# Two double norms of a three-block kernel: each square computed once, into a lent PSUM tile, both sums on VectorE

## The chip, the cores and the metric

The kernel runs on one core of one Trainium2 chip. The metric is the device time of one execution in microseconds, as the median of several runs; lower is better.

## The reference, cut to what matters

Three transformer-like blocks follow one another on 1024 positions of width 1024, in float32 (plus 16 meta positions in the first). Between blocks stand two norms in a row, with nothing between them: block 1 ends in a norm and block 2 begins with one, and block 2 ends in a norm and block 3 begins with one.

```python
h = h + jnp.square(jax.nn.relu(hn @ w_up[layer])) @ w_down[layer]
out = rms_norm(h, norm_final_w)
...
h = rmsnorm(x, ln1_g[l])
p = jnp.einsum('bsd,dn->bsn', h, w_in[l])
...
x = x + jnp.einsum('bsf,fd->bsd', hidden, w_down[l])
return rmsnorm(x, g_final)
...
h = rms_norm_3(x, norm1_pre) * (1.0 + scale1) + shift1
```

A norm divides by the root of the mean square over the 1024 features and multiplies by a gain g. Two in a row need two sums for each position: the sum of x squared, and the sum of (g x) squared, where g is the gain of the first of the two.

## The kernel before, in words

**Layout.** Features lie on the partitions, in eight tiles X[:, k, :] of 128 x 1024 (1024 positions in the free dimension). A weight block of 128 outputs is multiplied by all eight tiles. For precision each float32 operand is split into a high part and the rest: ScalarE rounds (`hh` for activations, `whi` for weights), VectorE or GpSimd subtracts (`hl`, `wlo`), and TensorE does three products per tile and half: whi with high, whi with low, wlo with high (L581, L582, L584). A product of eight tiles (`job`, L590) is 48 matmuls of 512 columns; one of four tiles, as in the second half of an MLP, is 24.

**PSUM.** There are three product tiles of 128 x 1024, `ps[0]` to `ps[2]`, taken in turn by `take` (L545), and a fourth, `misc`, for small things. `take` waits until the former holder of the slot is "free", that is, read by VectorE or ScalarE; it is called at the start of each product, ahead of its first matmul.

**Order.** Each engine has its own function with its program written out in order, and waits on the counts of the others. Weights come through a ring of four raw tiles on SyncE's queue; ScalarE casts a weight (`highs`, L1218) when the product two places earlier is done, and GpSimd makes the low part behind it (`lows`, L2605). `behind(name)` stands in ScalarE's and GpSimd's programs where that work is due.

**The two places.** Each of the first two MLPs ends in eight products of four tiles, one for each tile of X: dn7_0 to dn7_7 in block 1, fdn5_0 to fdn5_7 in block 2. VectorE adds product j to X (`to_x`, L2073). Then `on_last(j - 1)` follows on the engines, for the tile before:

- ScalarE (L1477, L1701): `high` makes hh (L1300), `square` writes x squared into T[0] (L1245; for tile 0 into T[2], L1237), and `square_b` writes (g x) squared into RT (L1253; for tile 0 into T[1], L1249).
- VectorE (L2148, L2418): `weigh` makes hl (L1871), and `square_sum` adds T[0] to T[2] (L1880, "acc").
- GpSimd (`square_sum_b`, L2624, drawn by L2616): adds RT to T[1] ("accb").

T[0] and RT have one buffer each: ScalarE's square k waits for acc k-1, and its scaled square k waits for accb k-1.

Behind the last product TensorE does the first projection of the next block (gg0 in block 2, zv0 in block 3: `job`, L865 and L1128), which waits tile by tile for hl. Then come `sums` (L667): for each of eight blocks of 128 positions, T[2] against a column of ones, and the same for T[1]. Float32 makes two matmuls of each, 16 for acc (L671) and 16 for accb (L676). The next projection (gv0, zv1) follows, and in it the factors are spread over the partitions (`spread_misc`).

Other norms (n1, n2, n4) have one sum and use `square` and `square_sum` without g.

Of the kernel before, what the change touches and what calls it, by code (L numbers as in the profile page):

```python
# [12 lines left out]
ACT = mybir.ActivationFunctionType  # L13
# [3 lines left out]
P = 128  # L17
# [227 lines left out]
def build(nc, d, out):  # L245
    ctx = ExitStack()
    with ctx:
# [43 lines left out]
        rms = const("rms", [P, 40])  # L291
        gprod = const("gprod", [P, 16])
        adat = const("adat", [P, 2, P])
        cols = const("cols", [P, NCOL])
# [241 lines left out]
        def tensor(e):  # L536
# [6 lines left out]
            one, two = rms[:, 8:16], rms[:, 32:40]  # L543

            def take(g):  # L545

                n = turn[0] % 3
                turn[0] += 1
                if held[n]:
                    q.wait_ge(*freed(held[n]))  # L550
                held[n], slot[g] = g, n
                return ps[n]
# [279 lines left out]
            def mlp(up, dn, sizes, htok, norm=None, nlast=None, step=None):  # L832

                def norm_in(k):
                    if k == 5:
                        spread_misc(norm + " sp", one, dv(norm + " r1"))

                n = 0
                for what, g, j in mlp_plan(up, dn, sizes):
                    if what == "up":  # L840
                        f = 4 * g + j
                        if norm or f > 2:
                            job(f"{up}{f}", hhs, hls, htok, 8, between=norm_in if norm and f == 1 else None)
                        if step:
                            step(n)
                        if norm and f == 0:
                            sums(norm, nlast)
                    elif norm or (g, j) != (len(sizes) - 1, 7):
                        s_ = 4 * (g % 2)
                        if norm or (g, j) != (len(sizes) - 1, 6):  # L850
                            job(f"{dn}{g}_{j}", ghs, gls, lambda k: [po(f"{up}lo{4 * g + k - s_}")], sizes[g], k0=s_)
                        else:
                            halves([f"{dn}{g}_6", f"{dn}{g}_7"], ghs, gls, lambda k, hf: [po(f"{up}lo{4 * g + k - s_}")], sizes[g], k0=s_, between=tail)
                        if step:
                            step(n)
                    n += 1

            mlp("up", "dn", [4] * 8, lambda k: [dv(f"hl2 {k}")], "n2", dv("n2 acc7"), step=row_step)
            row_step(-1)

# [5 lines left out]
            q.wait_ge(*dv("mod"))  # L866
            sums("n3", dv("n3 acc7"), po("n3 accb7"))
            job("gv0", hhs, hls, h3, 8, between=lambda k: k == 6 and spread_misc("n3 sp", two, dv("n3 r12"), dv("n3 s2")))
# [241 lines left out]
            for n, (what, g, j) in enumerate(mlp_plan("fup", "fdn", SIZES2)):  # L1110
                if what == "up":
                    m = FIRST2[g] + j
                    job(f"fupa{m}", hhs, hls, lambda k: [dv(f"hl4 {k}")], 8)
                    if m == 0:
                        q.wait_ge(*ac("rx rt"))
                        sums("n4", dv("n4 acc7"))
                    job(f"fupb{m}", hhs, hls, lambda k: [dv(f"hl4 {k}")], 8,
                        between=None if m else lambda k: k == 5 and spread_misc("n4 sp", one, dv("n4 r1")))
                else:
                    s_ = 4 * (g % 2)  # L1120
                    job(f"fdn{g}_{j}", ghs, gls, lambda k: [po(f"fuplo{FIRST2[g] + k - s_}")], SIZES2[g], k0=s_)
                row2_step(n)


            def h5(k):
                return [dv(f"hl5 {k}")]

            job("zv0", hhs, hls, h5, 8)  # L1128
            sums("n5", dv("n5 acc7"), po("n5 accb7"))
            job("zv1", hhs, hls, h5, 8, between=lambda k: k == 5 and spread_misc("n5 sp", two, dv("n5 r12"), dv("b43")))  # L1130
# [81 lines left out]
        def scalar(e):  # L1212
# [18 lines left out]

            def square(n, k, x, *tok, g=None):

                for t in tok:
                    q.wait_ge(*t)
                if k == 0:
                    e.activation(T[2][:], x, ACT.Square).then_inc(*ac.inc(f"{n} sq0"))  # L1237
                else:
                    if g is None:
                        if k > 2:  # L1240
                            q.wait_ge(*either(f"{n} acc{k - 2}"))
                    elif k > 1:
                        q.wait_ge(*either(f"{n} acc{k - 1}"))
                    b = T[(k - 1) % 2] if g is None else T[0]
                    e.activation(b[:], x, ACT.Square).then_inc(*ac.inc(f"{n} sq{k}"))  # L1245

            def square_b(n, k, x, g):
                if k == 0:
                    e.activation(T[1][:], x, ACT.Square, scale=g).then_inc(*ac.inc(f"{n} sqb0"))  # L1249
                else:  # L1250
                    if k > 1:
                        q.wait_ge(*po(f"{n} accb{k - 1}"))
                    e.activation(RT[:], x, ACT.Square, scale=g).then_inc(*ac.inc(f"{n} sqb{k}"))  # L1253

# [222 lines left out]
            def on_last3(m):  # L1477
                high(f"hh3 {m}", X[:, m, :], HH[:, m, :], dv(f"dn x7 {m}"), *([pe("up31")] if m == 0 else []), scale=gprod[:, m:m + 1])
                if m == 0:
                    q.wait_ge(*po("uplo31"))  # L1480
                square("n3", m, X[:, m, :], g=True)
                square_b("n3", m, X[:, m, :], col("norm_final", m))

# [4 lines left out]
            root("n3", 1024, double=True)  # L1488
            to_rt("n3", po("n3 accb7"))
            behind("gv0")  # L1490
# [210 lines left out]
            def on_last5(m):  # L1701
                high(f"hh5 {m}", X[:, m, :], HH[:, m, :], dv(f"fdn x5 {m}"), *([pe("fupb21")] if m == 0 else []), scale=gprod[:, 8 + m:9 + m])
                if m == 0:
                    q.wait_ge(*po("fuplo21"))
                square("n5", m, X[:, m, :], g=True)
                square_b("n5", m, X[:, m, :], col("g_final", m))

# [25 lines left out]
            root("n5", 1024, double=True)  # L1733
            to_rt("n5", po("n5 accb7"))
            behind("zv1")
# [115 lines left out]
        def vector(e):  # L1851
# [20 lines left out]

            def square_sum(n, k, g=None):
                if k == 0:
                    return
                b = T[(k - 1) % 2] if g is None else T[0]
                q.wait_ge(*ac(f"{n} sq{k}"))
                if k > 1:
                    q.wait_ge(*either(f"{n} acc{k - 1}"))
                e.tensor_tensor(T[2][:], T[2][:], b[:], ADD).then_inc(*dv.inc(f"{n} acc{k}"))  # L1880

# [31 lines left out]
            q.wait_ge(*dv.now())  # L1913
            tt(gprod[:, 0:8], col("norm_final", 0, 8), col("ln1", 0, 8), MUL, "gprod")
            q.wait_ge(*dma["meta"]("meta"))
            for k in range(8):
# [231 lines left out]
            def on_last3(m):  # L2148
                if m == 0:
                    q.wait_ge(*pe("up31"))  # L2150
                weigh("hl3", m, gprod[:, m:m + 1])
                square_sum("n3", m, g=True)

# [264 lines left out]
            def on_last5(m):  # L2418
                if m == 0:
                    q.wait_ge(*pe("fupb21"))  # L2420
                weigh("hl5", m, gprod[:, 8 + m:9 + m])
                square_sum("n5", m, g=True)

# [111 lines left out]
            for m in range(6):  # L2535
                square_sum("nm", m)
                if m == 0:
                    q.wait_ge(*pe("n5 one"))
                    for k in range(8):
                        q.wait_ge(*ac(f"n5 sqb7"))  # L2540
                        stt(X[:, k, :], X[:, k, :], col("g_final", k), ps[slot["n5 one"]][:], MUL, MUL, f"x5n {k}", *(("free n5 one",) if k == 7 else ()))
# [57 lines left out]
        def gpsimd(e):  # L2599
# [23 lines left out]

            def square_sum_b(n, k):  # L2624
                if k:
                    q.wait_ge(*ac(f"{n} sqb{k}"))
                    q.wait_ge(*po.now())
                    tt(T[1][:], T[1][:], RT[:], ADD, f"{n} accb{k}")

            def low(n, x, hi, dst, tok):  # L2630
# [45 lines left out]

            def mlp(up, dn, sizes, step=None, on_last=None, late=1):
                n = 0
                for what, g, j in mlp_plan(up, dn, sizes):
# [5 lines left out]
                    if what == "up" and 4 * g + j >= late:  # L2685
                        for f in (range(late + 1) if 4 * g + j == late else [4 * g + j]):
                            sl = 4 * (f // 4 % 2) + f % 4
                            low(f"{up}lo{f}", T[f % 3][:], GH[:, sl, :], GL[:, sl, :], ac(f"{up}hi{f}"))
                    elif on_last and g == len(sizes) - 1 and j:
                        on_last(j - 1)  # L2690
                if on_last:
                    on_last(7)

# [5 lines left out]

            mlp("up", "dn", [4] * 8, row_step, lambda m: square_sum_b("n3", m))  # L2700

# [73 lines left out]
            for n, (what, g, j) in enumerate(mlp_plan("fup", "fdn", SIZES2)):  # L2775
# [10 lines left out]
                else:  # L2786
                    behind(f"fdn{g}_{j}")
                    row2_step(n, f"fdn{g}_{j}")
                    if g == 5 and j:
                        square_sum_b("n5", j - 1)  # L2790
            square_sum_b("n5", 7)


# [382 lines left out]
```

## Time and profile before

| what | us |
|---|---|
| median of 3 runs (lowest, highest) | 3523.36 (3521.64, 3528.19) |
| the profiled execution | 3526.7 |
| its span, first to last instruction | 3523.8 |
| TensorE matmul busy | 3431.2 (97%) |
| VectorE busy | 1588.2 (45%) |
| ScalarE busy | 1002.8 (28%) |
| GpSimd busy | 1308.9 (37%) |

The mean granted clock of TensorE over the span is 0.987 of full speed. Matmuls are pipelined: the record of one of 512 columns lasts about 0.39 us, while starts are about 0.23 us apart. Busy time of TensorE is therefore no measure of what it could still gain; starts and idle times are. In the rows, "[1.81 <-DVE HL L1871]" means that the engine was idle for 1.81 us before this instruction and that VectorE's instruction of line 1871, which writes HL, released it. PEclk is the granted clock in a stretch as a share of full speed (2.4 GHz).

### The profile page before, as it was taken

What the parts mean: (1) busy time and instruction counts of PE and PEld (TensorE: products, weight loads), DVE (VectorE), ACT (ScalarE), POOL (GpSimd) and SP (SyncE); (2) the same over time, 40 slices, a digit from 0 to 9 for tenths busy, and PEclk for the clock granted to TensorE, in tenths of its full rate; (3) what the DMA queues carried; (4) which work ended last, traced back from release to release, by engine and by line L of the source; (5) the groups of instructions that cost most, each with busy time, mean ns of one, the idle gap of its engine ahead of it and who ended that gap; (6) DMA issues with size and microseconds to landing.
All of it is one profiled execution on the core that took longest, in us unless ns stands there. A gap on an engine that the chain in (4) does not pass through costs nothing.

```text
span 3523.8 us, 39083 instructions
## 1 busy us (share of the span) xinstructions
PE 3431.2 (97%) x16810; PEld 2792.9 (79%) x16810; DVE 1588.2 (45%) x1630; ACT 1002.8 (28%) x1457; POOL 1308.9 (37%) x682
## 2 busy tenths in 40 slices
PE   8999999999999999998999999999999999999997
PEld 6888888888888878765788888888877778888886
DVE  5553343333333468475455545445554531222224
ACT  5432221111111421475232222212422432222222
POOL 3112334444444423213324344344433543333333
PEclk9999999999999999999999999999999999999998
DMA  3112312222222211110212133132211111111113
GB/s 109 37 60 72 108 48 90 88 87 89 89 87 79 93 66 48 49 58 1 84 48 72 62 100 96 63 99 87 73 42 37 70 51 51 49 48 48 48 50 121
DMA packets 89432, 242.93 MB, mean 69 GB/s; under 512 B 13334, under 2 KB 20262, under 8 KB 89132
## 3 DMA queue, kind: packets, MB, share of 16 engines
q1 hardware_dynamic: 89260, 240.44, 20.6%
q8 instruction: 132, 2.16, 0.2%
q14 instruction: 40, 0.33, 0.0%
HBM read 222.40 MB, written 18.00 MB: 68 GB/s over the span
## 4 chain that ended last, share of the span: by engine, by line
PE 90%; DVE 5%; ACT 3%; POOL 2%; issue 0%; DMA 0%; SPq 0%; DVEq 0%; ACTq 0%
PE ps L581 27%; PE ps L582 27%; PE ps L584 27%; POOL wlo L2610 1%; PE ps L751 1%; PE ps L968 1%; DVE T L1855 1%; PE ps L1017 1%; PE ps L1001 1%; DVE P L2266 1%; ACT T L1554 0%; POOL GL L2616 0%; PE ps L954 0%; PE ps L932 0%; PE ps L609 0%; PE ps L611 0%
## 5 line engine op out<-in xcount | busy, mean ns | idle before, releaser
L2610 POOL TENSOR_TENSOR wlo<-raw,whi 128x1024 fp32r<-128x1024 f32 (+3 forms) x367 | 697.7, 1901 | 1669.1 <-ACT whi L1227 1669.1
L581 PE MATMUL ps<-HH,whi 128*128 128x512 f32 (+2 forms) x2736 | 1083.6, 396 | 20.2 <-POOL wlo L2610 7.3
L582 PE MATMUL ps<-HL,whi 128*128 128x512 f32 (+2 forms) x2736 | 1071.0, 391 | 0.0
L584 PE MATMUL ps<-HH,wlo 128*128 128x512 f32 (+2 forms) x2736 | 848.2, 391 | 0.0
L1227 ACT ACTIVATE whi<-raw 128x1024 fp32r<-128x1024 f32 (+3 forms) x367 | 309.8, 844 | 1645.9 <-PE ps L584 1453.3
L581 PEld LDWEIGHTS ps<-HH,whi 128*128 128x128 f32 (+2 forms) x2736 | 514.1, 188 | 134.1 <-issue 7.2
L584 PEld LDWEIGHTS ps<-HH,wlo 128*128 128x128 f32 (+2 forms) x2736 | 513.6, 188 | 112.3 <-issue 0.6
L582 PEld LDWEIGHTS ps<-HL,whi 128*128 128x128 f32 (+2 forms) x2736 | 514.5, 188 | 108.7 <-issue 2.0
L581 PE MATMUL ps<-GH,whi 128*128 128x512 f32 x1520 | 597.8, 393 | 2.0 <-POOL wlo L2610 2.0
L582 PE MATMUL ps<-GL,whi 128*128 128x512 f32 x1520 | 591.8, 389 | 0.0
L584 PE MATMUL ps<-GH,wlo 128*128 128x512 f32 x1520 | 468.5, 389 | 0.0
L1855 DVE TENSOR_TENSOR X<-ps,X 128x1024 f32<-128x1024 f32 (+1 forms) x186 | 225.0, 1211 | 487.4 <-PE ps L584 485.8
L581 PEld LDWEIGHTS ps<-GH,whi 128*128 128x128 f32 x1520 | 285.6, 188 | 61.4 <-issue 3.5
L584 PEld LDWEIGHTS ps<-GH,wlo 128*128 128x128 f32 x1520 | 285.4, 188 | 59.6
L582 PEld LDWEIGHTS ps<-GL,whi 128*128 128x128 f32 x1520 | 285.7, 188 | 57.0
L2616 POOL TENSOR_TENSOR GL<-T,GH 128x1024 fp32r<-128x1024 f32 x86 | 206.9, 2407 | 320.8 <-ACT GH L1437 210.9
L2096 DVE TENSOR_REDUCE adat<-raw 128x128 f32<-128x1024 f32 x92 | 186.3, 2025 | 248.3 <-POOL raw L2616 248.2
L1866 DVE TENSOR_TENSOR T<-ps,RT 128x1024 f32<-128x1024 f32 x72 | 88.2, 1225 | 306.8 <-PE ps L584 272.1
L1855 DVE TENSOR_TENSOR T<-ps,RT 128x1024 f32<-128x1024 f32 (+2 forms) x34 | 41.6, 1223 | 262.9 <-PE ps L584 251.1
L1858 DVE SCALAR_TENSOR_TENSOR T<-T,cols,T 128x1023 f32<-128x1023 f32 x88 | 127.7, 1451 | 62.1 <-ACT T L1682 60.5
L1437 ACT ACTIVATE GH<-T 128x1024 fp32r<-128x1024 f32 x64 | 67.9, 1061 | 258.0 <-DVE T L1855 258.0
L1855 DVE TENSOR_TENSOR T<-T 128x1024 f32<-128x1024 f32 (+3 forms) x74 | 118.5, 1601 | 40.7 <-ACT T L1429 39.6
(380 smaller groups left out, 3030.3 us busy)
## 6 DMA issues: line engine op xcount, KB each, us to landing
raw<-in_w_up SPq DMA_DIRECT2D x76, 512.0 KB, 3.3
raw<-in_w_in SPq DMA_DIRECT2D x70, 512.0 KB, 3.2
raw<-in_w_fc SPq DMA_DIRECT2D x64, 512.0 KB, 3.2
raw<-in_w_down SPq DMA_DIRECT2D x104, 256.0 KB, 2.7
raw<-in_w_ada SPq DMA_DIRECT2D x48, 512.0 KB, 3.4
raw<-in_w_fc SPq DMA_DIRECT2D x64, 256.0 KB, 2.7
X<-in_xT SPq DMA_DIRECT2D x16, 512.0 KB, 7.1
raw<-in_w_out SPq DMA_DIRECT2D x16, 512.0 KB, 3.2
```

Source lines behind the costliest of these rows:

```text
L581: e.matmul(o_[0:m, half(hf)], whi_[:, k, :], hi[k0 + k][:, half(hf)], start=first, stop=False)
L582: e.matmul(o_[0:m, half(hf)], whi_[:, k, :], lo[k0 + k][:, half(hf)], start=False, stop=False)
L584: i = e.matmul(o_[0:m, half(hf)], wlo_[:, k, :], hi[k0 + k][:, half(hf)], start=False, stop=last)
L751: i = e.matmul(o_[:, at_:at_ + 64].rearrange("p (n w) -> p n w", n=mv.shape[1]), keys[r_, t_, blk(c)], mv, start=True, stop=True)
L1227: e.activation(whi_of(name), raw_of(name), ACT.Copy).then_inc(*ac.inc("hi " + name))
L1437: e.activation(GH[:, sl, :], t[:], ACT.Copy).then_inc(*ac.inc(f"{up}hi{f}"))
L1855: e.tensor_tensor(o, a, b, op).then_inc(*dv.inc(*names))
L1858: e.scalar_tensor_tensor(out=o, in0=a, scalar=s_, in1=b, op0=op0, op1=op1).then_inc(*dv.inc(*names))
L1866: e.tensor_tensor(dst, ps[slot[g]][:], RT[:], MUL).then_inc(*dv.inc("free " + g, *names))
L2096: e.tensor_reduce(adat[:, f % 2, :], raw_of(name).rearrange("p (k m) -> p m k", k=8), AX.X, ADD).then_inc(*dv.inc("red " + name))
L2610: e.tensor_tensor(wlo_of(name), raw_of(name), whi_of(name).bitcast(F), SUB).then_inc(*po.inc("lo " + name))
L2616: e.tensor_tensor(o, a, b, op).then_inc(*po.inc(*names))
```

## The change

Each square is computed once. ScalarE writes x squared of tile 0 into T[2], and of tiles 1 to 7 into a PSUM tile (`square_off`); the scaled squares and their instructions go. VectorE makes both sums (`square_sums`): for tile 0 it writes g squared times T[2] into T[1]; for the others it adds the PSUM tile to T[2], and the PSUM tile times g squared to T[1] in one three-operand instruction. g squared comes from two small multiplications at the start. GpSimd does no additions for the double norms. The PSUM tile is one of the three product slots: `lend`, called ahead of the first of the eight last products, names the slot whose turn it is, and `take` skips it; `returned`, behind the eighth, gives it back with "n3 sq" or "n5 sq" as its holder, which is free when the last accb is done.

```diff
+        gsq = const("gsq", [P, 16])
...
+            lent = []
+
+            def lend(g):
+
+                lent.append(turn[0] % 3)
+                slot[g] = lent[0]
+
+            def returned(g):
+                held[lent.pop()] = g
+
             def take(g):
 
+                if turn[0] % 3 in lent:
+                    turn[0] += 1
                 n = turn[0] % 3
                 turn[0] += 1
                 if held[n]:
...
+                        if norm and (g, j) == (len(sizes) - 1, 0):
+                            lend("n3 sq")
...
             mlp("up", "dn", [4] * 8, lambda k: [dv(f"hl2 {k}")], "n2", dv("n2 acc7"), step=row_step)
+            returned("n3 sq")
             row_step(-1)
...
             job("gg0", hhs, hls, h3, 8)
             q.wait_ge(*dv("mod"))
-            sums("n3", dv("n3 acc7"), po("n3 accb7"))
+            sums("n3", dv("n3 acc7"), dv("n3 accb7"))
...
+                    if (g, j) == (5, 0):
+                        lend("n5 sq")
...
+            returned("n5 sq")
             job("zv0", hhs, hls, h5, 8)
-            sums("n5", dv("n5 acc7"), po("n5 accb7"))
+            sums("n5", dv("n5 acc7"), dv("n5 accb7"))
...
-            def square_b(n, k, x, g):
-                if k == 0:
-                    e.activation(T[1][:], x, ACT.Square, scale=g).then_inc(*ac.inc(f"{n} sqb0"))
-                else:
-                    if k > 1:
-                        q.wait_ge(*po(f"{n} accb{k - 1}"))
-                    e.activation(RT[:], x, ACT.Square, scale=g).then_inc(*ac.inc(f"{n} sqb{k}"))
+            def square_off(n, k, x):
+
+                if k > 1:
+                    q.wait_ge(*dv(f"{n} accb{k - 1}"))
+                e.activation(ps[slot[n + " sq"]][:] if k else T[2][:], x, ACT.Square).then_inc(*ac.inc(f"{n} sq{k}"))
...
-                square("n3", m, X[:, m, :], g=True)
-                square_b("n3", m, X[:, m, :], col("norm_final", m))
+                square_off("n3", m, X[:, m, :])
...
+            def square_sums(n, k, g2):
+
+                q.wait_ge(*ac(f"{n} sq{k}"))
+                if k == 0:
+                    e.tensor_scalar(T[1][:], T[2][:], g2, None, MUL).then_inc(*dv.inc(f"{n} accb0"))
+                else:
+                    x = ps[slot[n + " sq"]][:]
+                    q.wait_ge(*dv(f"{n} accb{k - 1}"))
+                    tt(T[2][:], x, T[2][:], ADD, f"{n} acc{k}")
+                    stt(T[1][:], x, g2, T[1][:], MUL, ADD, f"{n} accb{k}", *((f"free {n} sq",) if k == 7 else ()))
...
+            tt(gsq[:, 0:8], col("norm_final", 0, 8), col("norm_final", 0, 8), MUL, "gsq3")
+            tt(gsq[:, 8:16], col("g_final", 0, 8), col("g_final", 0, 8), MUL, "gsq5")
...
-                square_sum("n3", m, g=True)
+                square_sums("n3", m, gsq[:, m:m + 1])
...
-            def square_sum_b(n, k):
-                if k:
-                    q.wait_ge(*ac(f"{n} sqb{k}"))
-                    q.wait_ge(*po.now())
-                    tt(T[1][:], T[1][:], RT[:], ADD, f"{n} accb{k}")
...
-            mlp("up", "dn", [4] * 8, row_step, lambda m: square_sum_b("n3", m))
+            mlp("up", "dn", [4] * 8, row_step)
```

The places of n5 (the second) are changed in the same way as those of n3; the copy of the spread factors into RT (`to_rt`) no longer waits for GpSimd's last addition, and the later use of the first of the two norms in block 3 waits for "n5 sq7" instead of "n5 sqb7".

## Rows read from the trace of the kernel before

**Rows 1.** The page, the chain that ended last: share of the span by engine.

```profile
PE 90%; DVE 5%; ACT 3%; POOL 2%; issue 0%; DMA 0%; SPq 0%; DVEq 0%; ACTq 0%
```

**Rows 2.** Timeline, TensorE, first place: start us, us, engine, line, instruction.

```profile
1199.01 0.50 PE L581 MATMUL ps<-HH,whi 128*128 128x512 f32 x1 [1.81 <-DVE HL L1871]
...
1201.12 3.41 PE L671 MATMUL ps<-ones,T 128*128 128x1 f32 x16
1204.39 3.55 PE L676 MATMUL ps<-ones,T 128*128 128x1 f32 x16
1207.81 0.77 PE L581 MATMUL ps<-HH,whi 128*128 128x512 f32 x1
```

**Rows 3.** Timeline, TensorE, second place.

```profile
2523.74 0.50 PE L581 MATMUL ps<-HH,whi 128*128 128x512 f32 x1 [1.82 <-DVE HL L1871]
```

**Rows 4.** Timeline, ScalarE, first place.

```profile
1162.15 1.05 ACT L1245 ACTIVATE T<-X 128x1024 f32<-128x1024 f32 x1
...
1182.33 1.06 ACT L1227 ACTIVATE whi<-raw 128x1024 fp32r<-128x1024 f32 x1 [1.78 <-PE ps L584]
1183.30 1.14 ACT L1300 ACTIVATE HH<-X,gprod 128x1024 fp32r<-128x1024 f32 x1
...
1187.77 1.06 ACT L1227 ACTIVATE whi<-raw 128x1024 fp32r<-128x1024 f32 x1 [1.35 <-PE ps L584]
```

**Rows 5.** Stretch, start of gv0: PEclk is third from the end.

```profile
1212.00:1214.00 2.00, 2.00 (x7) 1.57 (x7) 0.00 (x0) 0.00 (x0) 0.00 (x0) 0.65 0.00 0
```

**Rows 6.** Timeline, VectorE, first place.

```profile
1160.51 1.22 DVE L1855 TENSOR_TENSOR X<-ps,X 128x1024 f32<-128x1024 f32 x1 [2.29 <-PE ps L584]
1162.36 1.31 DVE L1871 SCALAR_TENSOR_TENSOR HL<-X,gprod,HH 128x1024 fp32r<-128x1024 f32 x1 [0.62 <-ACT HH L1300]
1163.59 1.21 DVE L1880 TENSOR_TENSOR T<-T,T 128x1024 f32<-128x1024 f32 x1
...
1185.41 2.18 DVE L1871 SCALAR_TENSOR_TENSOR HL<-X,gprod,HH 128x1024 fp32r<-128x1024 f32 x1
1187.52 3.42 DVE L1880 TENSOR_TENSOR T<-T,T 128x1024 f32<-128x1024 f32 x1
...
1197.67 1.28 DVE L1871 SCALAR_TENSOR_TENSOR HL<-X,gprod,HH 128x1024 fp32r<-128x1024 f32 x1
```

**Rows 7.** Groups by form, VectorE: count, then busy us, mean ns of one.

```profile
L1880 DVE TENSOR_TENSOR T<-T,T 128x1024 f32<-128x1024 f32 x43 | 73.9, 1720 | 40.4 <-ACT T L1788 36.4 <-ACT T L1245 4.0
...
L1858 DVE SCALAR_TENSOR_TENSOR T<-ps,RT 128x1024 f32<-128x1024 f32 x32 | 39.0, 1218 | 64.2 <-PE ps L584 56.4 <-ACT RT L1266 7.7
...
L1855 DVE TENSOR_TENSOR T<-T,ps 128x1024 f32<-128x1024 f32 x6 | 7.3, 1222 | 29.4 <-ACT T L1495 15.6 <-PE ps L584 13.8
```

**Rows 8.** Timeline, GpSimd, first place.

```profile
1183.47 3.04 POOL L2610 TENSOR_TENSOR wlo<-raw,whi 128x1024 fp32r<-128x1024 f32 x1 [0.32 <-ACT whi L1227]
...
1199.84 2.46 POOL L2616 TENSOR_TENSOR T<-T,RT 128x1024 f32<-128x1024 f32 x1 [3.29 <-ACT RT L1253]
```

**Rows 9.** Timeline and stretches, TensorE after two other waits.

```profile
2688.19 0.76 PE L581 MATMUL ps<-HH,whi 128*128 128x512 f32 x1 [6.33 <-DVE HL L1855]
...
2832.76 0.77 PE L581 MATMUL ps<-HH,whi 128*128 128x512 f32 x1 [4.14 <-POOL wlo L2610]
...
2690.00:2692.00 2.00, 2.00 (x7) 1.58 (x6) 2.00 (x2) 0.10 (x1) 2.00 (x2) 0.66 0.00 0
...
2838.00:2840.00 2.00, 2.00 (x10) 1.63 (x9) 2.00 (x2) 0.59 (x1) 0.29 (x1) 0.96 0.00 0
```

**Rows 10.** Timeline and stretch, TensorE, the sums of an earlier norm.

```profile
487.24 1.84 PE L671 MATMUL ps<-ones,T 128*128 128x1 f32 x16
...
488.00:490.00 2.00, 2.00 (x15) 1.81 (x15) 0.00 (x0) 1.97 (x3) 1.37 (x1) 1.00 0.68 244
```

**Rows 11.** Timeline, VectorE, the kernel's start.

```profile
3.92 0.17 DVE L1855 TENSOR_TENSOR gprod<-cols 128x8 f32<-128x8 f32 x1
5.01 1.20 DVE L1917 TENSOR_SCALAR TM<-XM,cols 128x16 f32<-128x16 f32 x8 [0.92 <-DMA XM<-in_metaT]
```

More of the change, by code:

```diff
@@ L1230, in behind, with square @@
                 highs(widx[name] + 2)
-            def square(n, k, x, *tok, g=None):
+            def square(n, k, x, *tok):
                 for t in tok:
@@ L1238, in square @@
                 else:
[L1239 to L1245, printed above, removed]
-            def square_b(n, k, x, g):
-                if k == 0:
-                    e.activation(T[1][:], x, ACT.Square, scale=g).then_inc(*ac.inc(f"{n} sqb0"))
-                else:
-                    if k > 1:
-                        q.wait_ge(*po(f"{n} accb{k - 1}"))
-                    e.activation(RT[:], x, ACT.Square, scale=g).then_inc(*ac.inc(f"{n} sqb{k}"))
+                    if k > 2:
+                        q.wait_ge(*either(f"{n} acc{k - 2}"))
+                    e.activation(T[(k - 1) % 2][:], x, ACT.Square).then_inc(*ac.inc(f"{n} sq{k}"))
+            def square_off(n, k, x):
+                if k > 1:
+                    q.wait_ge(*dv(f"{n} accb{k - 1}"))
+                e.activation(ps[slot[n + " sq"]][:] if k else T[2][:], x, ACT.Square).then_inc(*ac.inc(f"{n} sq{k}"))
             def root(n, width, double=False):
@@ L1488, in scalar @@
             root("n3", 1024, double=True)
-            to_rt("n3", po("n3 accb7"))
+            to_rt("n3")
             behind("gv0")
@@ L1704, in on_last5 @@
                     q.wait_ge(*po("fuplo21"))
-                square("n5", m, X[:, m, :], g=True)
-                square_b("n5", m, X[:, m, :], col("g_final", m))
+                square_off("n5", m, X[:, m, :])
             q.wait_ge(*dv("gains"))
@@ L1733, in scalar @@
             root("n5", 1024, double=True)
-            to_rt("n5", po("n5 accb7"))
+            to_rt("n5")
             behind("zv1")
@@ L1871, in low, with square_sum @@
                 e.scalar_tensor_tensor(out=dst, in0=x, scalar=g, in1=hi.bitcast(F), op0=MUL, op1=SUB).then_inc(*dv.inc(n))
-            def square_sum(n, k, g=None):
+            def square_sum(n, k):
                 if k == 0:
                     return
-                b = T[(k - 1) % 2] if g is None else T[0]
                 q.wait_ge(*ac(f"{n} sq{k}"))
@@ L1879, in square_sum @@
                     q.wait_ge(*either(f"{n} acc{k - 1}"))
-                e.tensor_tensor(T[2][:], T[2][:], b[:], ADD).then_inc(*dv.inc(f"{n} acc{k}"))
+                e.tensor_tensor(T[2][:], T[2][:], T[(k - 1) % 2][:], ADD).then_inc(*dv.inc(f"{n} acc{k}"))
+            def square_sums(n, k, g2):
[7 more added lines that the diff above has]
+                    stt(T[1][:], x, g2, T[1][:], MUL, ADD, f"{n} accb{k}", *((f"free {n} sq",) if k == 7 else ()))
             def factors(n, double=False):
@@ L2421, in on_last5 @@
                 weigh("hl5", m, gprod[:, 8 + m:9 + m])
-                square_sum("n5", m, g=True)
+                square_sums("n5", m, gsq[:, 8 + m:9 + m])
             for n, (what, g, j) in enumerate(mlp_plan("fup", "fdn", SIZES2)):
@@ L2539, in vector @@
                     for k in range(8):
-                        q.wait_ge(*ac(f"n5 sqb7"))
+                        q.wait_ge(*ac("n5 sq7"))
                         stt(X[:, k, :], X[:, k, :], col("g_final", k), ps[slot["n5 one"]][:], MUL, MUL, f"x5n {k}", *(("free n5 one",) if k == 7 else ()))
@@ L2675, in row_tile, with mlp @@
                 tt(w_, w_, vec.unsqueeze(2).broadcast_to([P, 8, P]), MUL, name)
-            def mlp(up, dn, sizes, step=None, on_last=None, late=1):
+            def mlp(up, dn, sizes, step=None, late=1):
                 n = 0
@@ L2688, in mlp @@
                             low(f"{up}lo{f}", T[f % 3][:], GH[:, sl, :], GL[:, sl, :], ac(f"{up}hi{f}"))
[L2689 to L2692, printed above, removed]
             def row_step(n, name):
@@ L2788, in gpsimd @@
                     row2_step(n, f"fdn{g}_{j}")
-                    if g == 5 and j:
-                        square_sum_b("n5", j - 1)
-            square_sum_b("n5", 7)
             for m in range(4):
```

## The prediction

> **What bounds the kernel now.** I read the page first, then timelines of single engines in the two places that the diff touches, then granted clocks there. The chain that ended last is TensorE for 90% [rows 1], so an edit counts by what it does to TensorE's start times. The two places are the last eight products before gg0 (first MLP) and before zv0 (second MLP); they run alike to 0.01 us (gg0 and zv0 each lose 1.81 or 1.82 us to a wait for the last HL, [rows 2, 3]), so I work out the first and count it twice.
>
> In the first place a product takes 5.44 us of TensorE (ScalarE's casts behind two product ends start 5.44 us apart, 1182.33 and 1187.77, [rows 4]). The second of these is the end of dn7_7. There gg0 begins at once: it takes hl3 0 to 6 as they come, and stops only before its last eighth, for hl3 7, until 1199.01 [rows 2]. Eight tiles of 1.36 us make 10.88 us for gg0 at the full clock. Then come the two sums, 3.41 and 3.55 us for 16 matmuls each, and gv0 starts at 1207.81 [rows 2]. From the end of dn7_7 to gv0 that is 20.04 us. The reader should also see that the clock is at its lower level (1.2 GHz) by then, and that in the stretch 1212 to 1214 it is 0.65 on average [rows 5], so it came back at 1213.4: gv0 ran 5.6 us at half speed, another 2.8 us lost.
>
> **The wait that the change adds.** This is my main step. `lend` is called ahead of dn7_0 and sets aside L, the slot whose turn it is. dn7_0 skips it and takes L+1, dn7_1 takes L+2, dn7_2 finds the turn at L again and skips; so the even products have L+1, the odd ones L+2, and after dn7_7 the turn stands at L. `returned` now writes "n3 sq" as the holder of L, and the next `take` is gg0's: it gets L and waits for "free n3 sq", which VectorE signals with its last addition, accb7. gg0 could start on seven eighths of its work before; now none of it starts until VectorE is done. Queued behind that wait on TensorE is everything. zv0 has the same place after fdn5_7.
>
> **When accb7 is done.** A product's share on VectorE is X (1.22), hl, and now acc and accb. Starts of before are 1160.51 (X), 1162.36 (hl), 1163.59 (acc) [rows 6], so acc starts 3.08 after X. The new pair reads PSUM. No row has this pair; the nearest are a sum of T and PSUM (1222 ns) and a three-operand form of PSUM and SBUF (1218 ns); the upper end is the mean of the old addition with both inputs in SBUF, 1720 ns [rows 7]; nothing below 1.2 is seen at this size. I take 1.22, since the operands' places are those; starts follow 1.14 apart. That gives 3.08 + 2 x 1.14 = 5.36 against 5.44: VectorE just keeps up through job 5. Squares on ScalarE fit: one of 1.05 [rows 4] instead of that and a scaled one, and it waits for the accb of the product before, done by then; writing PSUM instead of SBUF I take at the same 1.05, with 0.1 either way.
>
> At 1182.33 the cast is of a 1024-wide weight (1.06) and hh5 follows at 1183.30 for 1.14 [rows 4], so hl5 starts at 1184.5. GpSimd makes the low half of that weight from 1183.47 for 3.04 us [rows 8]; beside it hl takes 2.18 instead of 1.31 [rows 6]. hl5 is over at 1186.7, acc5 at 1187.85, accb5 at 1189.0. X7, ready at 1187.77, runs 1189.0 to 1190.2. hl6, again beside a 1024-wide low half, ends 1192.35; acc6 1193.5; accb6 1194.6; hl7 1195.9 (its 1.28 is seen at 1197.67); acc7 and accb7 end 1198.2 (sq7 waits for accb6 and is over by 1195.8). gg0 starts at 1198.3, **10.55 us after dn7_7**.
>
> A rule of the Trainium skill ("VectorE: DVE Perf Modes", section on the TRN2 errata) gives VectorE 62 more cycles of fixed cost for a PSUM source than for an SBUF one, some 65 ns; by that the four instructions behind dn7_7 that newly read PSUM would put gg0 0.26 us later. The rows have 1222 ns [rows 7] against 1.21 us for the old addition with GpSimd idle [rows 6], so I leave it out.
>
> **TensorE's clock.** A wait of 6.33 us ended at 2688.19; the stretch 2690 to 2692 has 0.66, so the full level was back at 2691.4, 3.2 us after work resumed. A wait before 2832.76 was followed by full level at 2838.2 (0.96 in 2838 to 2840), 5.4 us later [rows 9]. Both waits had let the clock fall; one of 10.55 us will too. gg0 thus runs its first 3.2 to 5.4 us at half speed and loses 1.6 to 2.7; I take 2.15. It loses no time before its last eighth, since hl3 7 is older than accb7.
>
> The sums then begin at the full clock. At that clock 16 such matmuls take 1.84 us, and the clock stayed full over them [rows 10]; two sums are 3.7 us instead of 6.7 (from 1201.12 to 1207.81). But 3.7 us of one-column work behind one another is not seen at the full clock, and before, the clock fell around the wait that ended at 1199.01 and stayed down through all 6.7 us of it. I hold it likelier that the clock falls in or right behind them, take 4.5 us for both, and leave gv0 its old loss of 2.8.
>
> **The sum.** 10.55 + 10.88 + 2.15 + 4.5 = 28.1 us against 20.04: **+8.0 us per place, +16 for two**. Behind gv0 and zv1 TensorE is dense again and nothing else changed, so the delay reaches the end whole.
>
> **What is removed or costs nothing.** GpSimd loses 14 additions of up to 3.4 us, ScalarE 16 squares. GpSimd's last addition ended at 1199.84 + 2.46 = 1202.30, before the second sum at 1204.39, so nobody waited for it: worth 0. It does take the 3.42 us stretches [rows 6] out of VectorE's old additions; that is in the timeline above, and without the slot's wait hl3 7 would come at 1195.9, in time for gg0. The products have two slots instead of three: product j+2 needs X(j), read 1.22 us after j's end, and starts 5.44 after it; hidden as long as VectorE is under 4.2 us late (1.3 at X7). The two small multiplications for gsq fall in VectorE's 0.92 us of idle time before the metadata [rows 11] and cost nothing; were that cover gone they would cost 0.34. No DMA is added or moved, and SP's queue waits for nothing new.
>
> **Rivals.**
> (a) *Wait, but no fall in the sums.* All as above, but the sums take 3.7 and gv0 loses nothing: 27.3 against 20.04 + 2.8 = 22.8, +4.4 each, +9: 3532. For it: 1.84 us of sums left the clock alone [rows 10]. Against: the dip of before outlasted all the sums. The Trainium skill ("TensorE: Matmul & The Clock Gate", Part 1) has the gate follow how busy the engine has been; it doesn't settle how one-column work counts.
> (b) *Faster: gg0 does not meet the lent slot.* Its place is one call of `take`: if my count of turns is off by one, or the wait has long passed, gg0 starts at 1187.77 and finds hl3 7 in time. It saves the 1.81, the 0.7 by which the dipped clock stretched its last tile (1199.01 to 1201.12 is 2.11 against 1.36), and 2.2 in the sums: -4.7 each, -9 in all (3514), and down to -17 if the clock doesn't fall. It decides once gg0 starts before 1190. For it: the change frees VectorE from GpSimd. Against: the count above.
> (c) *VectorE falls behind.* Spare room per product is 0.08 us. If the PSUM pair cost 1.7 each, VectorE would lose 1.0 at each of five products and accb7 would end some 5 to 6 us later: 3549 or more. It decides from 1.26 us per instruction on. The rows [rows 7] speak against it.
> (d) *It does little:* the delay is taken up by a later wait, or the clock's phases fall well. 3523 plus or minus 5.
>
> **How the numbers follow.** The profiled execution had 3526.7 us with a span of 3523.8, 3.3 above the median 3523.36; the change is added to the median. Forecast: 3523.4 + 16 = 3539. Chances: forecast 0.55, (a) 0.27, (b) 0.07, (c) 0.05, (d) 0.06. The range takes in the forecast and (a) with the bounds of the clock's loss (1.6 to 2.7) and of the sums (3.7 to 6.7): those give 3531 to 3545, and 2 us at either end are left for the runs' own scatter: 3529 to 3547. About 0.2% (7 us) is what a measurement of this kernel can tell from no change; (a) is just above it. So faster 0.07, same 0.07, slower 0.86.
>
> **What would show it.** In the profile after: gg0's and zv0's first matmul behind an idle time of 10 to 11 us put down to VectorE's three-operand instruction of T from PSUM; no wait of 1.8 us inside gg0; low clock at the start of gg0; the first 16 one-column matmuls near 1.84 us; old-form additions of 3.4 us gone and the new ones near 1.22 us; product ends still 5.44 apart. It is wrong if gg0's first matmul comes within 2 us of dn7_7's end, or if new waits stand between the eight products.

## The result and the profile of the changed kernel

The changed kernel takes **3545.88 us** (median of 6 runs, 3544.17 to 3550.91) against 3525.14 us for the kernel before beside it (6 runs, 3521.64 to 3528.75). The ratio is 1.0058, 95% interval 1.0048 to 1.0069: **20.7 us slower**. The profiled execution took 3546.35 us with a span of 3544.6 us and a mean granted clock of 0.984 (before: 0.987).

The page of the changed kernel, its first line and the chain by engine, which answers to [rows 1]:

```profile
PE 3432.6 (97%) x16810; PEld 2790.9 (79%) x16810; DVE 1587.2 (45%) x1648; ACT 986.2 (28%) x1441; POOL 1264.1 (36%) x668
...
PE 91%; DVE 4%; ACT 3%; POOL 1%; DMA 0%; issue 0%; SPq 0%; DVEq 0%; ACTq 0%
```

The bound is the same. What is new is at the top of TensorE's waits (what was waited for, us in all, times, longest):

```profile
PE ps L594 <- DVE T L1869: 21.4, 2, 10.7
```

L1869 is the helper of VectorE's three-operand instruction, here the last of the new additions, accb7. Two waits of 10.7 us: one per place.

The timeline of TensorE in the changed kernel (start, us, engine, line, instruction, idle time before it and who ended it), the first place, a point between the places, and the second place; it answers to [rows 2, 3]:

```profile
1193.76 0.61 PE L597 MATMUL ps<-GH,wlo 128*128 128x512 f32 x2
1205.07 0.80 PE L594 MATMUL ps<-HH,whi 128*128 128x512 f32 x1 [10.70 <-DVE T L1869]
1205.66 0.63 PE L595 MATMUL ps<-HL,whi 128*128 128x512 f32 x1
...
1210.22 0.40 PE L594 MATMUL ps<-HH,whi 128*128 128x512 f32 x1
...
1218.39 1.84 PE L684 MATMUL ps<-ones,T 128*128 128x1 f32 x16
1220.09 1.93 PE L689 MATMUL ps<-ones,T 128*128 128x1 f32 x16
1221.88 0.49 PE L594 MATMUL ps<-HH,whi 128*128 128x512 f32 x1
...
2346.05 0.50 PE L594 MATMUL ps<-HH,whi 128*128 128x512 f32 x1 [2.02 <-POOL wlo L2633]
...
2536.13 0.79 PE L594 MATMUL ps<-HH,whi 128*128 128x512 f32 x1 [10.70 <-DVE T L1869]
...
2549.54 1.84 PE L684 MATMUL ps<-ones,T 128*128 128x1 f32 x16
2551.24 1.93 PE L689 MATMUL ps<-ones,T 128*128 128x1 f32 x16
2553.03 0.49 PE L594 MATMUL ps<-HH,whi 128*128 128x512 f32 x1
```

dn7_7 ends at 1194.37, gg0 starts at 1205.07. Its first matmuls last 0.63 us in the record, against 0.39 at the full clock. They overlap, so their starts tell more: these are 0.43 apart and later 0.23, which is half the pace. From 1210.22 on they are at full speed again. Then both sums run at 1.84 and 1.93 us, and gv0 starts at 1221.88: 27.5 us from the end of dn7_7, where by the same record (its last matmul) it was 20.1 before.

Granted clock in the changed kernel (stretch, length, busy time of PE, PEld, DVE, ACT, POOL, then PEclk, DMA share, GB/s), around the restart, over the start of gv0, and between the places; the third line answers to [rows 5]:

```profile
1206.00:1208.00 2.00, 2.00 (x6) 1.52 (x5) 0.00 (x0) 0.00 (x0) 0.00 (x0) 0.50 0.00 0
...
1220.00:1222.00 2.00, 2.00 (x20) 2.00 (x20) 0.00 (x0) 0.00 (x0) 2.00 (x1) 1.00 0.00 0
1222.00:1224.00 2.00, 2.00 (x10) 1.64 (x10) 1.07 (x6) 0.57 (x2) 0.13 (x1) 1.00 0.00 0
...
2346.00:2348.00 2.00, 1.95 (x6) 1.57 (x7) 0.12 (x1) 0.00 (x0) 2.00 (x2) 0.67 0.24 96
2348.00:2350.00 2.00, 2.00 (x7) 1.52 (x6) 1.86 (x1) 0.00 (x0) 2.00 (x1) 0.50 0.00 0
```

0.50 is the lower level, 1.2 GHz. It holds behind the new wait, and, unlike before, not over the sums or at the start of gv0.

VectorE in the changed kernel from product 7 to gg0, which answers to [rows 6]:

```profile
1178.09 1.23 DVE L1866 TENSOR_TENSOR X<-ps,X 128x1024 f32<-128x1024 f32 x1
1179.93 1.32 DVE L1882 SCALAR_TENSOR_TENSOR HL<-X,gprod,HH 128x1024 fp32r<-128x1024 f32 x1 [0.61 <-ACT HH L1313]
1181.17 1.21 DVE L1866 TENSOR_TENSOR T<-ps,T 128x1024 f32<-128x1024 f32 x1
1182.31 1.27 DVE L1869 SCALAR_TENSOR_TENSOR T<-ps,gsq,T 128x1024 f32<-128x1024 f32 x1
1183.53 1.22 DVE L1866 TENSOR_TENSOR X<-ps,X 128x1024 f32<-128x1024 f32 x1
...
1191.24 2.42 DVE L1882 SCALAR_TENSOR_TENSOR HL<-X,gprod,HH 128x1024 fp32r<-128x1024 f32 x1 [1.04 <-ACT HH L1313]
...
1194.71 1.27 DVE L1869 SCALAR_TENSOR_TENSOR T<-ps,gsq,T 128x1024 f32<-128x1024 f32 x1
1195.90 1.21 DVE L1866 TENSOR_TENSOR X<-ps,X 128x1024 f32<-128x1024 f32 x1
1197.14 1.90 DVE L1882 SCALAR_TENSOR_TENSOR HL<-X,gprod,HH 128x1024 fp32r<-128x1024 f32 x1
...
1201.40 1.28 DVE L1882 SCALAR_TENSOR_TENSOR HL<-X,gprod,HH 128x1024 fp32r<-128x1024 f32 x1
1202.61 1.22 DVE L1866 TENSOR_TENSOR T<-ps,T 128x1024 f32<-128x1024 f32 x1
1203.74 1.27 DVE L1869 SCALAR_TENSOR_TENSOR T<-ps,gsq,T 128x1024 f32<-128x1024 f32 x1
```

X to X is 5.44 us, TensorE's own period. VectorE's own share is hardly less: 1.84 from X to hl, 1.24 to acc, 1.14 to accb and 1.19 to the next X (the last from 1194.71 to 1195.90, where TensorE's product had been ready since 1194.37) make 5.41. So VectorE keeps up with almost nothing to spare. The two stretches beside GpSimd's low half (2.42 and 1.90) put it behind, and hl7 comes at 1201.40. Without the new wait that would have been early enough: gg0 needs it 9.5 us after its start.

**Where the difference lies.** I matched the starts of TensorE's matmuls by their number in the two traces and took how much later each stands in the changed kernel. The shift grows by 6.7 us up to the end of dn7_7, by 4.8 in the first place, 1.5 up to the second, 4.9 there and 2.3 behind it: 20.2 in all. So in this pair of traces the places hold only 9.7 us of it. Whether the other 10.5 belong to the change was the question for the experiments.

### The profile page after: what moved, and what is told of

It reads as the page before. It is cut to its first block, busy times and chain, and to the rows that moved or that the text cites. A ratio compares the mean times of both kernels' runs of the same rounds, so it can differ in the third digit from the quotient of the medians.

```text
span 3544.6 us, 39056 instructions
## 1 busy us (share of the span) xinstructions
PE 3432.6 (97%) x16810; PEld 2790.9 (79%) x16810; DVE 1587.2 (45%) x1648; ACT 986.2 (28%) x1441; POOL 1264.1 (36%) x668
## 3 DMA queue, kind: packets, MB, share of 16 engines
q1 hardware_dynamic: 89260, 240.44, 20.7%
## 4 chain that ended last, share of the span: by engine, by line
PE 91%; DVE 4%; ACT 3%; POOL 1%; DMA 0%; issue 0%; SPq 0%; DVEq 0%; ACTq 0%
PE ps L594 28%; PE ps L595 27%; PE ps L597 27%; PE ps L764 1%; DVE T L1866 1%; POOL wlo L2633 1%; PE ps L984 1%; PE ps L622 1%; PE ps L1033 1%; PE ps L624 1%; PE ps L623 1%; PE ps L1017 1%; DVE T L1869 1%; DVE P L2289 1%; ACT T L1566 0%; PE ps L970 0%
## 5 line engine op out<-in xcount | busy, mean ns | idle before, releaser
L1869 DVE SCALAR_TENSOR_TENSOR T<-T,cols,T 128x1023 f32<-128x1023 f32 x88 | 127.2, 1445 | 62.1 <-ACT T L1694 60.5
```

Of the source, the lines that this page charges most:

```text
L1869: e.scalar_tensor_tensor(out=o, in0=a, scalar=s_, in1=b, op0=op0, op1=op1).then_inc(*dv.inc(*names))
```

## The experiments

My theory going in: the wait of gg0 and zv0 for the lent slot, with the clock's restart behind it, is the whole cause; everything else in the change is worth nothing or a little. Rivals: the start of the kernel (the two small multiplications) carries some of the 6.7 us; one of the places alone does the harm; the PSUM additions do. The small tables give medians, and the ratio to the kernel before from the same chip, with its 95% interval.

**e1: the lent slot is passed on.** One line, so that gg0 and zv0 don't get it. They take the slot of the last product but one, the next projection takes that of the last product, and the third projection gets the lent one:

```diff
             def returned(g):
                 held[lent.pop()] = g
+                turn[0] += 1
```

> The changed kernel, but the turn moves on by one when the slot is given back, so gg0 and zv0 take the slot that the next to last product has left and the third projection gets the lent one. Nothing is left out of the computation. My theory (the wait ahead of gg0 and zv0 is what costs): no idle time before gg0's and zv0's first matmul, hl7 in time for the last eighth, sums near 1.84 us for 16 matmuls; 8 to 17 us under the kernel before, so 3508 to 3517. Rival (about 10 us of the 20.7 come from somewhere else, where TensorE's clock dips at about 43 and 200 us in the changed kernel's trace): the wait is gone all the same, but 10 us remain, 3518 to 3527. Rival (two slots for the last products cost something): product ends more than 5.44 us apart.

**e2: the wait alone, in the kernel before.** gg0 and zv0 wait for the last HL in place of their last eighth; nothing of the change is in it:

```diff
+            q.wait_ge(*dv("hl3 7"))
             job("gg0", hhs, hls, h3, 8)
...
+            q.wait_ge(*dv("hl5 7"))
             job("zv0", hhs, hls, h5, 8)
```

> The kernel before with one thing added: gg0 and zv0 don't begin until hl7 of their norm is done. Nothing else of the change. My theory: TensorE idles about 11.2 us at each place, the clock falls, 10 to 20 us slower than the kernel before. Rival (the cost of the change lies in its other parts): within 4 us of the kernel before.

**e3: the constant gsq alone, in the kernel before.**

```diff
+        gsq = const("gsq", [P, 16])
...
+            tt(gsq[:, 0:8], col("norm_final", 0, 8), col("norm_final", 0, 8), MUL, "gsq3")
+            tt(gsq[:, 8:16], col("g_final", 0, 8), col("g_final", 0, 8), MUL, "gsq5")
```

> The kernel before with the small constant and its two multiplications at the start and nothing else of the change. My theory: no difference, 3525 plus or minus 3. Rival (a systematic cost at the start, by which the changed kernel's trace is already 6.7 us late at the end of dn7_7): 3530 to 3535, with low clock near 43 and 200 us.

**e4: the changed kernel again**, on the same chip as these.

> The changed kernel once more, for a second trace of it. If the low clock at 42.7 to 46.1 and 199.7 to 206.5 us is a matter of chance, it stands elsewhere or not at all in this one, and the total is 3541 to 3551 all the same only if other dips take their place; if it belongs to the change, it stands at the same times. Idle before gg0 and zv0 10.7 us each again.

Measured, with 19 runs of the kernel before at 3526.74:

| run | median us | runs | ratio |
|---|---|---|---|
| e1 slot passed on | 3515.93 | 9 | 0.9975 [0.9965, 0.9985] |
| e2 only the wait | 3539.47 | 5 | 1.0049 [1.0037, 1.0062] |
| e3 only gsq | 3526.61 | 11 | 1.0002 [0.9993, 1.0011] |
| e4 changed again | 3544.16 | 5 | 1.0054 [1.0042, 1.0067] |

One line turns 17 to 21 us lost into 10.8 us won: **e1 beats both kernels**. TensorE in e1, the same place:

```profile
1187.52 0.62 PE L598 MATMUL ps<-GH,wlo 128*128 128x512 f32 x2
1187.97 0.39 PE L595 MATMUL ps<-HH,whi 128*128 128x512 f32 x1
...
1199.00 1.95 PE L685 MATMUL ps<-ones,T 128*128 128x1 f32 x16
1200.81 1.93 PE L690 MATMUL ps<-ones,T 128*128 128x1 f32 x16
1202.59 0.48 PE L595 MATMUL ps<-HH,whi 128*128 128x512 f32 x1
```

gg0 follows dn7_7 with no idle time, gets hl7 in time (VectorE starts it at 1195.22) and waits nowhere; from the end of dn7_7 (1188.14) to gv0 it is 14.5 us, against 20.1 before and 27.5 in the changed kernel. Granted clock there in e1 (columns as above):

```profile
1196.00:1200.00 4.00, 4.00 (x23) 3.16 (x22) 2.95 (x4) 1.14 (x2) 0.00 (x0) 1.00 0.00 0
1200.00:1204.00 4.00, 4.00 (x30) 3.78 (x30) 0.53 (x3) 0.66 (x3) 2.35 (x1) 0.92 0.03 6
1204.00:1206.00 2.00, 2.00 (x6) 1.54 (x6) 0.55 (x3) 0.08 (x1) 0.00 (x0) 0.50 0.00 0
1206.00:1208.00 2.00, 2.00 (x9) 1.60 (x8) 0.00 (x0) 0.00 (x0) 0.00 (x0) 0.81 0.00 0
```

The clock falls at 1203.4, behind the sums and not in them, for 3.4 us.

e2 has the wait without any other part of the change. TensorE in e2:

```profile
1205.78 0.80 PE L581 MATMUL ps<-HH,whi 128*128 128x512 f32 x1 [11.17 <-DVE HL L1873]
...
1219.48 1.84 PE L671 MATMUL ps<-ones,T 128*128 128x1 f32 x16
1221.18 3.02 PE L676 MATMUL ps<-ones,T 128*128 128x1 f32 x16
```

The same idle time (11.2 at both places), the same restart, and most of the loss: 12.7 us by the medians. Its five runs lie in two groups, three at 3538.4 to 3539.5 and two at 3547.3 and 3547.7, so its median is a coarse number. The trace is of the run at 3547.3, and in it the clock fell again over the second sum (the 3.02 above). e3 shows nothing: the multiplications are free.

**e5 and e6: the wait at one place alone.** As e1, with the slot passed on only behind the second place (e5 keeps the wait ahead of gg0) or only behind the first (e6 keeps it ahead of zv0):

```diff
                 held[lent.pop()] = g
+                turn[0] += g == "n5 sq"
```

(e6 has "n3 sq" there.)

> The changed kernel with the turn moved on at the second place alone, so that gg0 waits for the lent slot and zv0 doesn't. My theory (the two waits cost alike and add up): half way between e1 (3516) and the changed kernel (3544 to 3546), so 3528 to 3533, with one idle time of 10.7 us. Rival (the first wait also shifts the clock's dips of everything behind it, and costs more than the second): 3535 or more here, and under 3526 in the reverse run.

> The reverse: zv0 waits for the lent slot, gg0 doesn't. My theory: 3528 to 3533 again. Rival: under 3526.

**e7: no slot is lent.** The squares of tiles 1 to 7 go to T[0] in SBUF, both sums are VectorE's from there, and the products turn over three slots:

```diff
-                            lend("n3 sq")
...
-            returned("n3 sq")
...
-                e.activation(ps[slot[n + " sq"]][:] if k else T[2][:], x, ACT.Square).then_inc(*ac.inc(f"{n} sq{k}"))
+                e.activation(T[0][:] if k else T[2][:], x, ACT.Square).then_inc(*ac.inc(f"{n} sq{k}"))
...
-                    x = ps[slot[n + " sq"]][:]
+                    x = T[0][:]
```

> The changed kernel without lending: the squares of tiles 1 to 7 go into T[0] in SBUF, VectorE makes both sums from there, and the products have all three slots. Computes the same. My theory (what gains in e1 is that GpSimd's additions and the last wait for hl7 are gone, not the PSUM place): no wait ahead of gg0, 3515 to 3521, VectorE's additions a little slower where GpSimd makes a low half at the same time. Rival (the PSUM place is needed, since two SBUF inputs collide with GpSimd): hl7 late again, 3522 or more, additions over 1.5 us on average.

**e8: e1 with a shorter wait**, for the last HL but one:

```diff
+            q.wait_ge(*dv("hl3 6"))
             job("gg0", hhs, hls, h3, 8)
...
+            q.wait_ge(*dv("hl5 6"))
             job("zv0", hhs, hls, h5, 8)
```

> e1 with a shorter wait: gg0 and zv0 begin when hl6 is done, which by e1's trace leaves TensorE idle for some 5 us at each place instead of 10.7. Theory (the cost is the idle time itself plus a step when the clock falls, since half speed after restart is the same for either): 3516 + 2 x 5 + 2 x 2 = 3530, between 3526 and 3533. Rival (cost is in proportion to the idle time alone, 28 us for 21.4): 3529 too, so the totals don't tell, but the clock does: it stays full over a 5 us wait. What tells is the share at half speed behind the restart.

Measured, with 33 runs of the kernel before at 3524.63:

| run | median us | runs | ratio |
|---|---|---|---|
| e5 wait at the first place | 3530.72 | 11 | 1.0019 [1.0010, 1.0028] |
| e6 wait at the second place | 3531.16 | 11 | 1.0021 [1.0012, 1.0030] |
| e7 no lent slot | 3519.99 | 11 | 0.9988 [0.9979, 0.9997] |
| e8 shorter wait at both | 3532.63 | 11 | 1.0020 [1.0011, 1.0029] |

e5 and e6 each stand half way between e1 (3515.9) and the changed kernel (3544 to 3546): **by the medians each wait costs about 15 us against e1, and the two add up**.

In e7 VectorE's pair reads SBUF, with GpSimd idle beside it, and takes the same time as from PSUM:

```profile
1178.73 1.21 DVE L1860 TENSOR_TENSOR T<-T,T 128x1024 f32<-128x1024 f32 x1
1179.87 1.27 DVE L1863 SCALAR_TENSOR_TENSOR T<-T,gsq,T 128x1024 f32<-128x1024 f32 x1
```

So PSUM as such buys VectorE no time here. I had expected additions a little slower beside a low half of GpSimd; that case did not arise, since in neither place of e7 did one of these additions run beside one. And e7, without PSUM, is still faster than the kernel before, though only just (its interval ends at 0.9997). Its trace agrees at the two places: they are 4.8 and 6.9 us cheaper than in the first trace of the kernel before. So the sums' move off GpSimd is enough for a gain. Why e7's median lies 4 us above e1's stays open; the runs come from two chips, and in e7's one trace 9.7 us of delay were there ahead of the first place, where the kernels don't differ.

TensorE in e8, where the wait is 4.72 us at each place:

```profile
1199.98 0.79 PE L595 MATMUL ps<-HH,whi 128*128 128x512 f32 x1 [4.72 <-DVE HL L1885]
1200.57 0.63 PE L596 MATMUL ps<-HL,whi 128*128 128x512 f32 x1
...
1205.20 0.40 PE L595 MATMUL ps<-HH,whi 128*128 128x512 f32 x1
```

The clock falls in a wait of 4.72 us too, against the rival of e8, and the restart lasts as long (1199.98 to 1205.20) as behind 10.70 us (1205.07 to 1210.22). Over all traces it is 4.8 and 5.1 us behind the two waits of 4.72, and 4.1 to 5.8 behind the eight of 10.7. So a wait costs its length and one restart, whichever of the two lengths. By the shifts of TensorE's matmuls a place of e8 is 5.6 us later than in e1, and a place of the changed kernel 12.4 (average of six): the idle time and 0.9 or 1.7 us, since e1 has a short fall of its own behind the sums, worth 1.7. The medians give more, 8 and 15 us a place. In the traces the rest lies outside the places: e8's is 7.1 us later than e1's ahead of the first place, where the two kernels are alike, 1.7 between the places and 2.1 behind them. How much of that the waits cause is not shown; single traces are no measure of it, since these two are 22 us apart where the medians are 16.7.

**e9 to e12: the kernels again, one run each**, to see what repeats: the kernel before (e9, e10), the changed one (e11), e1 (e12).

> The kernel before, for a second trace. Question: the traces of the changed kernel were 3.2 and 6.7 us later than the first trace of the kernel before at the end of dn7_7, where the change has done nothing yet. Theory (chance of the clock in the first 210 us): this trace too can be up to 7 us late there, with dips near 42 or 200 us, and its total is 3521 to 3532 all the same. Rival (the start belongs to the change): within 1 us of the first trace at dn7_7. Behind zv1 I expect the low-clock stretches of block 3 as in the first trace (6.8 us near the third block's longest wait), and not the longer ones of 10.2 us that every trace with a wait ahead of zv0 had.

> As e9_before_again: a third trace of the kernel before, 0 to 7 us late at the end of dn7_7 if the start is chance, within 1 us if it belongs to the change.

> A third trace of the changed kernel. Theory: late by anything from 0 to 7 us at the end of dn7_7; +5 to +6 at each place; +2.3 behind zv1 again, since that part repeats in every trace with the wait ahead of zv0. Rival (all of it chance): no 2.3 behind zv1.

> A second trace of e1. Theory: 5 to 8 us won at each place, nothing (under 0.7 us) lost behind zv1, start anything from 0 to 7 us late.

The times were 3524.97, 3523.41, 3544.77 and 3515.36, beside 3525.71 for a run of the kernel before. What counts are the shifts of TensorE's matmuls (us) against the first trace of the kernel before, worked out as above; each column is the growth in that part:

| trace | up to dn7_7 | place 1 | between | place 2 | behind | total |
|---|---|---|---|---|---|---|
| before, e9 | +2.0 | 0.0 | -1.5 | -4.7 | +2.3 | -1.8 |
| before, e10 | +6.7 | -4.7 | -2.1 | -4.7 | +2.2 | -2.4 |
| changed, first | +6.7 | +4.8 | +1.5 | +4.9 | +2.3 | +20.2 |
| changed, e4 | +3.2 | +6.0 | +2.9 | +4.9 | +2.4 | +19.3 |
| changed, e11 | +4.3 | +4.9 | +1.0 | +8.4 | -0.4 | +18.2 |
| e1 | +0.5 | -6.7 | -0.7 | -6.9 | +0.1 | -13.7 |
| e12 (as e1) | +2.9 | -6.7 | -0.4 | -6.9 | -0.2 | -11.3 |

The kernel before has the 6.7 us at the start in e10 and the 2.3 behind the second place in e9 and e10. So neither belongs to the change. I had tied the latter to the wait ahead of zv0, in what I expected of e9 and of e11, and both were misses: e9 has the 2.3 without that wait, and e11 lacks it with the wait. The first trace of the kernel before had simply been free of both.

It had been unlucky in the places instead. TensorE in e10, first place, to be read against [rows 2]:

```profile
1205.73 0.50 PE L581 MATMUL ps<-HH,whi 128*128 128x512 f32 x1 [1.80 <-DVE HL L1871]
...
1207.22 1.84 PE L671 MATMUL ps<-ones,T 128*128 128x1 f32 x16
1209.09 1.95 PE L676 MATMUL ps<-ones,T 128*128 128x1 f32 x16
```

The same kernel, the same wait of 1.8 us, and here the clock stays full over the sums; only a short fall behind them is left. Such a place is 4.7 us cheaper. Of the six places in three traces of the kernel before, three went each way (both places of the first trace and the first of e9 were dear). On average over three traces each, the two places together are at -4.7 before and +11.3 in the changed kernel: **16.0 us apart**. All else is at +3.3 and +7.9: 4.6 us apart. Of these 4.6, 1.8 are ahead of the first place and 3.0 between the places.

2.5 of the 3.0 arise at one instruction, the one near 2346 us above. TensorE waits there for the low half of a weight, and the weight itself comes late. ScalarE's cast of it, in the changed kernel and then in the first trace of the kernel before:

```profile
2342.51 1.06 ACT L1246 ACTIVATE whi<-raw 128x1024 fp32r<-128x1024 f32 x1 [6.49 <-DMA raw<-in_w_up]
...
2331.14 1.06 ACT L1227 ACTIVATE whi<-raw 128x1024 fp32r<-128x1024 f32 x1 [5.70 <-DMA raw<-in_w_up]
```

TensorE's wait is 1.85 to 2.02 us in all nine traces of kernels in which VectorE makes both sums (the changed kernel, e1, e5 to e8, e12), and 0.91 to 1.20 us in all five of the others (the kernel before, e2, e3). So about 0.8 us belongs to the change, and e1 has it too; why the weight lands later no run shows. The other 1.7 us are the clock: it falls behind this wait in the three traces of the changed kernel (two stretches stand above), in e5 and in e8, which all have a wait ahead of gg0, and not in e1, e12, e6 and e7, which have none. e2 has a wait ahead of gg0 and no fall there, but its wait near 2346 is a short one (1.20). So the fall goes with the two waits together in these traces; that one brings about the other is not shown.

## Why the prediction was right, point by point

The forecast was 3539 us, +16; measured +20.7 (e4: +17.4). Sign and mechanism hold. For the places the sum gives the right total by two errors that cancel, which is luck, and it has nothing for the 4 to 5 us outside them.

- **The lent slot falls to gg0 and zv0.** Shown: 10.70 us of idle time put down to VectorE's last addition, at both places, and one line that hands the slot to another job takes it all away (e1).
- **When accb7 is done.** 10.55 worked out, 10.70 measured. The parts: the pair 1.22 each, measured 1.21 and 1.27; 5.36 per product for VectorE, measured 5.41 of the 5.44 there are, nearly at the limit; hl beside the low half 2.18, measured 2.42 and 1.90. The rule of the Trainium skill ("VectorE: DVE Perf Modes", section on the TRN2 errata), by which a PSUM source costs 62 cycles more than an SBUF one, was left out of the sum, and the traces don't bear it out: e7 has 1.21 and 1.27 us with all tiles in SBUF, the same as from PSUM. No extra of 65 ns is seen.
- **The restart.** 2.15 was taken, with bounds of 1.6 and 2.7; gg0 took 13.32 us from start to sums, 2.44 over 10.88.
- **The sums and gv0.** This is the term that was mis-sized, in two halves. I had the clock fall in or behind the sums (4.5 us, and gv0 keeping a loss of 2.8); in the profiled execution the sums took 3.49 and gv0 lost nothing, at both places, which is rival (a) (27.3 us worked out from the end of dn7_7 to gv0, 27.5 measured). In the six places of the three changed traces the clock fell around the sums in two (e4 for 3.4 us, e11 for 6.8). So the truth per place lies between forecast and rival: against the first trace of before, +4.8 and +4.9 in the profiled execution and 5.6 on average over the six, not the +8.0 of the forecast and not the +4.4 of rival (a).
- **What made up for it** is the other side of the same coin: I took the 20.04 us of one trace of the kernel before as its price, and half its places are 4.7 us cheaper. The two errors cancel: 16.0 on average for the two places. That the sum has exactly this number is luck.
- **"The delay reaches the end whole", and nothing else changes.** The delay does, but something else changed. By three traces each 4.6 us more come from elsewhere: 1.8 ahead of the first place, where only the multiplications for gsq differ and e3 shows them free, so I take this as chance; and 2.5 at the wait near 2346 us, 0.8 of it a longer wait that comes with the change and 1.7 a fall of the clock behind it. By these traces it is this that puts the result above the forecast.
- **GpSimd's removal worth 0.** True only beside the wait, as the prediction has it: the wait covers hl7. Without the wait the change brings 10.8 us (e1), the -9 of rival (b) and a little over. So it holds a gain of some 5 us per place and a wait that costs some 15, by the medians.
- **The multiplications for gsq, the squares on ScalarE, two slots for the products:** free, as said. e3 is at 1.0002; the products stay 5.44 us apart.

## What to carry to other kernels

A buffer lent out of a rotation and given back at its head puts its last reader in front of the next job. Pass it to the back of the rotation instead: that one line was worth 28 to 30 us here. In these traces a TensorE wait of 4.7 or 10.7 us cost its length plus one restart at the lower level, which took 2.0 to 2.9 us; by the medians of whole runs such a wait cost 8 and 15 us. And with effects of 0.3% read several traces of each kernel: the clock's falls differ from one execution of the same program to the next, and a single trace taken as the price of a stretch can be off by 5 us.

## What the runs showed of the hardware that was not expected

- At the same instruction, behind the same wait of 1.79 to 1.82 us, the granted clock fell in three of six places of the kernel before and stayed full in the other three.
- 32 one-column matmuls in a row (3.5 to 3.6 us) ran at the full clock in all four places of e1 and e12, and the clock fell right behind them, for 3.4 us, each time. The same happened in the first place of e6 and the second of e7, but not everywhere: in the second place of e5, which has no wait either, the clock stayed full (1.00 in 2540 to 2544), and in the first of e7 it fell during the second sum. In the changed kernel, where a restart came some 8 us earlier, it fell in two of six.
- One weight's DMA, near 2346 us and ahead of the second place, kept TensorE waiting about 0.8 us longer in all nine traces of kernels with VectorE's sums than in the five others, though the change adds and moves no DMA.
- With GpSimd idle, VectorE's 128x1024 additions take the same from PSUM as from SBUF (1.21, and 1.27 us for the three-operand form). ScalarE's square is a little faster into PSUM than into SBUF. ScalarE in the changed kernel:

```profile
1163.41 1.05 ACT L1266 ACTIVATE T<-X 128x1024 f32<-128x1024 f32 x1
...
1168.85 1.00 ACT L1266 ACTIVATE ps<-X 128x1024 f32<-128x1024 f32 x1
```
